# Order of a few steps in the RWKV-7 and sparse-attention stages of a decoder-layer kernel

## The reference, cut to what matters

```python
def step(S, inp):
    r_t, w_t, k_t, v_t, kk_t, a_t = inp
    sa = jnp.einsum('bhij,bhj->bhi', S, -kk_t)
    S = (S * w_t[:, :, None, :] + sa[..., None] * (kk_t * a_t)[:, :, None, :]
         + v_t[..., None] * k_t[:, :, None, :])
    return S, jnp.einsum('bhij,bhj->bhi', S, r_t)
...
_, sel = lax.top_k(index, topk)
...
logits = jnp.einsum('bthd,btkhd->bthk', q, k_sel).astype(jnp.float32) * HEAD_DIM ** -0.5 + bias
```

## Time and profile before

| | us |
|---|---|
| median of 3 runs | 1629.0 |
| lowest and highest | 1625.16, 1631.47 |
| the profiled execution: its own time | 1633.64 |
| its span on the engines | 1631.9 |
| TensorE matmul busy | 1535.6 |
| VectorE busy | 1140.8 |
| ScalarE busy | 730.0 |
| GpSimd busy | 269.3 |

### The profile page before, as it was taken

One profiled execution on the slowest core, in us unless ns is written; L12 is line 12 of the kernel. 1 busy time (PEld: TensorE's weight loads), 2 busy tenths in 40 slices (PEclk: granted clock), 3 DMA queues, 4 the chain that ended last, 5 costly groups with the idle time before them and its releaser, 6 DMA issues.

```text
span 1631.9 us, 41517 instructions
## 1 busy us (share of the span) xinstructions
PE 1535.6 (94%) x17667; PEld 1197.5 (73%) x17667; DVE 1140.8 (70%) x2453; ACT 730.0 (45%) x1286; POOL 269.3 (17%) x188
## 2 busy tenths in 40 slices
PE   6999999999999797899779999999999999999998
PEld 4586666664667576677657976888888888888887
DVE  3699999988767756877632789988888886100056
ACT  4743232113678555666553224555555554311100
POOL 2422111012211111212123000000000002322100
PEclk9999999998999798998999999999999999999999
DMA  8223122325530203000105211111222222821001
GB/s 300 62 79 131 53 71 71 101 92 167 158 105 21 73 10 125 23 23 23 56 11 189 90 45 52 53 53 53 83 101 79 79 92 94 319 78 53 27 30 79
DMA packets 53874, 138.84 MB, mean 85 GB/s; under 512 B 17594, under 2 KB 24506, under 8 KB 46362
## 3 DMA queue, kind: packets, MB, share of 16 engines
q1 hardware_dynamic: 52602, 135.13, 24.3%
q0 software_dynamic: 1088, 1.05, 0.2%
HBM read 106.44 MB, written 29.72 MB: 83 GB/s over the span
## 4 chain that ended last, share of the span: by engine, by line
PE 82%; DVE 9%; issue 3%; ACT 3%; SPq 2%; DMA 1%; DVEq 0%; ACTq 0%
PE bank L2618 78%; PE bank L2785 2%; DVE arena L3001 1%; DVE arena L2281 1%; PE bank L1079 1%; SPq L972 1%; PE bank L1024 1%; DVE arena L2315 0%; DMA arena<-oht 0%; PE bank L1984 0%; SPq L831 0%; DVE arena L1650 0%; SPq L835 0%; DVE arena L2999 0%; DVE arena L2293 0%
## 5 line engine op out<-in xcount | busy, mean ns | idle before, releaser
L2618 PE MATMUL bank<-arena 64*64 64x64 f32 (+11 forms) x16960 | 1452.4, 278 | 83.9 <-issue 18.2
L2618 PEld LDWEIGHTS bank<-arena 128*128 128x128 f16 (+7 forms) x16960 | 1120.5, 120 | 413.8 <-issue 125.8
L3041 DVE TENSOR_SCALAR_CACHE_REDUCE arena<-arena 128x384 bf16<-128x384 f32 (+6 forms) x231 | 196.9, 916 | 1.2
L3170 POOL TENSOR_TENSOR arena<-arena 128x2048 f16<-128x2048 f32 x32 | 130.3, 4074 | 398.4 <-ACT arena L2828 386.2
L2827 ACT ACTIVATE arena<-arena 128x2048 f16<-128x2048 f32 x32 | 61.0, 1906 | 160.7 <-PE bank L2618 134.4
L2844 ACT ACTIVATE arena<-bank 128x352 f32<-128x352 f32 x72 | 33.1, 462 | 183.9 <-PE bank L2618 183.9
L1831 POOL TENSOR_TENSOR arena<-arena 128x512 f32<-128x512 f32 x40 | 54.4, 1367 | 241.9 <-PE bank L2618 107.9
L2475 POOL COPY arena<-arena 128x2 f32<-128x2 f32 x22 | 22.4, 1019 | 426.5 <-DVE arena L2415 326.7
L2446 DVE COPY arena<-bank 128x256 f32<-128x256 f32 x4 | 1.7, 424 | 121.5 <-PE bank L2618 121.5
L2138 ACT ACTIVATE arena<-arena 128x1024 f16<-128x1024 f32 x76 | 65.9, 938 | 35.7 <-DVEq L2306 35.7
L2193 ACT ACTIVATE arena<-bank 128x264 f32<-128x264 f32 x114 | 43.4, 389 | 79.0 <-PE bank L2618 79.0
(11 more groups left out here) (290 smaller groups left out, 1431.8 us busy)
## 6 DMA issues: line engine op xcount, KB each, us to landing
arena<-slabs SPq DMA_DIRECT2D x53, 1024.0 KB, 4.9
arena<-kcache SPq DMA_DIRECT2D x32, 256.0 KB, 2.9
arena<-vcache SPq DMA_DIRECT2D x32, 256.0 KB, 2.9
prw<-arena SPq DMA_DIRECT2D x42, 176.0 KB, 1.9
hd<-arena SPq DMA_DIRECT2D x11, 528.0 KB, 2.7
arena<-xt SPq DMA_DIRECT2D x8, 528.0 KB, 11.3
x1d<-arena SPq DMA_DIRECT2D x8, 512.0 KB, 2.6
arena<-x1d SPq DMA_DIRECT2D x1, 4096.0 KB, 19.1
```

What stands on the lines that cost most here:

```text
L2618: return nc.tensor.matmul(out, lhsT, rhs, start=start, stop=stop, skip_group_check=True)
L3041: last = dve.tensor_scalar(junk, a, s, None, op, ALU.add, accum_out=cnt[:, k:k + 1])
L3170: pool.tensor_tensor(WL[r].rearrange("p a b -> p (a b)"), STG[s], WH[r].rearrange("p a b -> p (a b)"), ALU.subtract).then_inc(slab_lo, 1)
```

## The change

Five edits. (1) In `RW_PERIOD`, `lx` of level 3 (item k-2) stands ahead of `fin` 0 (item k-1) where it stood behind it. (2) The sample steps of periods 1 and 2 are placed later: `zscan`, `zsquare` with `zln`, and `zkm` each move behind the neighbouring level step, `zexp` and `zbo` go behind `lp` 3 of period 2, and `zfin` behind `lx` 3. (3) `zout` moves from behind `lx` 1 of period 2 to behind `bo` of period 3, and the 16 stores on SP from behind the raw transfer of item 2 to behind that of item 3. (4) The mask of query block 7 is made in two pieces, three instructions at `svalues` 0 and two at `svalues` 1; that of block 6 stays. (5) SP reads the 16 page numbers of a round into registers ahead of the wait for that round's buffers, and the loop that issues the transfers uses these registers.

```diff
+MASK_STEPS = {("slogits", 0): (6, range(5)), ("svalues", 0): (7, range(3)), ("svalues", 1): (7, range(3, 5))}
...
-    ("exp", "a", 1), ("norm", "a"), ("lp", "b", 3), ("km", "a"), ("ch", "c", 1), ("rstd", "d"), ("split", "t", 1), ("fin", "a", 0), ("lx", "b", 3),
+    ("exp", "a", 1), ("norm", "a"), ("lp", "b", 3), ("km", "a"), ("ch", "c", 1), ("rstd", "d"), ("split", "t", 1), ("lx", "b", 3), ("fin", "a", 0),
...
-    ("zgate", "z0"), ("bv", "a"), ("y", "c"), ("split", "s", 0), ("ch", "c", 7), ("out", "c", 0), ("lp", "a", 1), ("ss", "p"), ("zscan", "z0"),
-    ("ln", "p"), ("cen", "c"), ("out", "c", 1), ("lx", "a", 1), ("scan", "p"), ("gh", "b"), ("zsquare", "z0"), ("zln", "z0"), ("var", "c"),
-    ("out", "c", 2), ("lp", "a", 2), ("exp", "p", 0), ("zkm", "z0"), ("ry", "b"), ("ch", "b", 0), ("lx", "a", 2), ("zbo", "z0"), ("zexp", "z0"))
-RW_SAMPLE = {(2, "lp", 3): ("zfin",), (2, "bo"): ("ztl",), ...
-             (2, "lx", 1): ("zout",), (2, "gh"): ("zvar",), ...
+    ("zgate", "z0"), ("bv", "a"), ("y", "c"), ("split", "s", 0), ("ch", "c", 7), ("out", "c", 0), ("lp", "a", 1), ("ss", "p"),
+    ("ln", "p"), ("cen", "c"), ("out", "c", 1), ("lx", "a", 1), ("zscan", "z0"), ("scan", "p"), ("gh", "b"), ("var", "c"),
+    ("out", "c", 2), ("lp", "a", 2), ("zsquare", "z0"), ("zln", "z0"), ("exp", "p", 0), ("ry", "b"), ("ch", "b", 0), ("lx", "a", 2), ("zkm", "z0"))
+RW_SAMPLE = {(2, "lp", 3): ("zexp", "zbo"), (2, "lx", 3): ("zfin",), (2, "bo"): ("ztl",), ...
+             (3, "bo"): ("zout",), (2, "gh"): ("zvar",), ...
...
-                if n == 2:
+                if n == 3:
                     emptied(sp, ("zout", 0, HP - 1))
...
+        def page_numbers(sp, r):
+            at = [PG * (4 * (r % 2) + q) + g for q in range(4) for g in range(PG)]
+            return [sp.value_load(PTB[0:1, n:n + 1], min_val=0, max_val=NPOOL - 1) for n in at]
...
             for r, read in enumerate((("slg", 0, 0), ("slg", 1, 0), ("sav", 0))):
+                pages = page_numbers(sp, r + 1)
                 sp.wait_ge(filled, plan.number(read) + 1)
                 for q in range(4):
-                    load_pages(sp, r + 1, q)
+                    load_pages(sp, r + 1, q, pages)
...
-                if kind == "slogits":
-                    for n in range(5):
-                        mask(LATE_MASKS[u] - 2, n, MASKTMP)
-                    dve.sem_inc(mask_ready, 1)
+                if (kind, u) in MASK_STEPS:
+                    j, steps = MASK_STEPS[kind, u]
+                    for n in steps:
+                        mask(j - 2, n, MASKTMP)
+                    if n == 4:
+                        dve.sem_inc(mask_ready, 1)
```

More of the change, by code:

```diff
@@ L2599, in _ @@
                     sp.wait_ge(pt_in, 16)
+                    pages = page_numbers(sp, 0)
                 if w >= SL_OUT - NRING:
[L2601 removed]
+                    load_pages(sp, 0, w % NRING, pages)
             for q in range(4):
```

10 lines of the change are left out of this document (4 added, 6 removed).

## The result

The changed kernel takes 1619.2 us (median of 7 runs, 1614.5 to 1621.4) against 1629.0 us (7 runs, 1625.2 to 1631.5): a ratio of 0.9936, 95% interval 0.9921 to 0.9950, which is 10.4 us less, between 8.1 and 12.9. The forecast was 1612 us, 17 us less, in a range of 1605 to 1620. So the sign and the range held, and the gain came out at six tenths of what the sum promised. Its profiled execution took 1621.4 us, with a span of 1619.7.

A forecast was written before the change was run, and what follows sets the result against it. PE, busy for 94% of the span, was taken as the bound, so only its waits or lower clock could be won. Terms 2.8 + 1.6 + 2.3 - 0.1 + 4.2 + 5.2 + 1.2 = 17.2 us gave 1612 us, range 1605 to 1620.

The forecast's parts named there:

- Pages: Attention, ahead of `svalues` 1: PE's wait for value pages goes, 2.8 us, or 0 if the transfers were the limit.
- The term for the clock: At `svalues` 1, behind the page wait: PE's work at the lower clock returns to the higher, 1.6 us, bounds 0 and 1.6.
- Mask: Attention, unit 10: PE's wait for DVE shrinks by 2.3 us (bounds 1.7 and 3.3), less 0.1 charged behind `svalues` 0.
- Turn to period 2: Recurrence, sample steps regrouped and edit 1: level 4 of item 0 starts 4.2 us earlier, bounds 2.6 and 5.
- Stores and period 3: Edit 3, and edit 1 in period 3: 3.26 us raw-transfer wait plus 2.0 us at `zout`; 5.2 us, bounds 3.3 and 6.
- Swap in periods 4 to 8: Edit 1 ahead of level 4: 0.9 us kept in period 6, 0.3 in period 5; 1.2 us, bounds 0 and 3.6.
- DVE takes it back: Rival: in the recurrence PE then waits for DVE at the next `ch`, `fin` or `km`; 10.4 us gain, 1619; chance 0.18.
- The clock gives more: Rival: fewer waits keep PE at the higher clock in the recurrence, 5 us in its first half; 1606; chance 0.08.
- the case of the lower bounds: Rival "Nothing measurable": transfers bound round 3 and ACT the turn, leaving 6.6 us, 1622; chance 0.08.
- The test that I had set myself: Recurrence, 530 to 865 us: prediction wrong if granted clock changes by more than 0.05 or the stretch shrinks under 8 us.

The follow-up runs named there:

- small_pool: Changed kernel with GpSimd's masking products of levels 3 to 5 cut to one of eight pairs, so the recurrence is not computed: 0.9919 of the kernel before.
- swap: Kernel before with edit 1 alone (level update ahead of `fin` 0): 0.9974 of the kernel before, 4.2 us less.
- no_stores: Changed kernel with edit 3 undone (`zout` and the 16 stores back ahead of the raw transfer of item 3): 0.9941 of the kernel before.
- stores: Kernel before with edit 3 alone (`zout` and the 16 state stores moved behind the raw transfer of item 3): 1.0003 of the kernel before.

## Why the prediction was right in sign and too large in size

**Pages: the wait right, the clock not.** The wait is gone, and SP issues its 16 transfers of round 3 in 9.5 us, 0.59 us apart (forecast 0.63). SP's timeline of the changed kernel and PE's at `svalues` 1:

```profile
435.23 9.49 SPq L840 DMA_DIRECT2D arena<-vcache  x16
...
451.87 7.79 PE L2625 MATMUL bank<-arena 64*128 64x256 f32 x74
```

The transfers kept up. The term for the clock, 1.6 us, is where this step failed: the lower level did leave `svalues` 1, but it came only in three of five traces with the wait, and all eight kernels with edit 5 have it behind a later wait instead, where the same 42 matmuls take 5.6 us or more in place of 4.09. Net of that the term is about nothing. Alone the edit gained 4.9 us (2.6 to 7.3), so the total does not contradict it.

**Mask: right in total, by another split.** The units up to 14 came 2.8 us earlier in six of the kernels with this edit, for a forecast of 2.3 less 0.1. Only 1.2 us of it is idle time, about half of what was forecast, and 1.6 us is PE's clock behind the wait, which the term had only in its upper bound. That the two make up the 2.3 us is partly luck. Only the changed kernel and `small_pool` have 1.1, because their `slogits` 1 ran at the lower clock. PE's wait in unit 10 is 1.44 us in place of 2.34, not below 0.7 as announced. And 0.7 us is given back behind `svalues` 0, seven times the 0.1 charged:

```profile
414.72 1.29 PE L2625 MATMUL bank<-arena 128*64 128x128 f32 x14 [1.44 <-issue]
...
438.26 1.36 PE L2625 MATMUL bank<-arena 64*128 64x256 f32 x12 [0.71 <-DVE arena L3161]
```

The second place had been named (softmax scaling behind the first pieces), within its bounds of 0 and 1.0. The first piece took 5.0 us (432.76 to 437.79), between the 5.4 and the 4.3 that the prediction had for it, since a product of GpSimd (432.31 to 433.60) ran beside its first instruction here, too. Both attention edits together give 4.8 to 4.9 us at `sm` 0 in five of the kernels, for 6.6 in the sum: what is missing is about the 1.6 of clock.

**Turn to period 2: mis-sized, 3.4 in place of 4.2 us.** Level 4 of item 0 starts 18.0 us behind PE's first row after `sm` 0 (538.79 to 556.76), for 21.4 before (543.38 to 564.76). The wait of 3.09 us ahead of level 4 fell to 0.79, and the other waits on the way, 4.5 us in four before, are 4.5 us in five now. So waits give 2.3 of the 3.4 us; the rest is PE's clock, 0.85 in place of 0.79 from `sm` 0 to `xi` 1. PE's timeline and then DVE's and GpSimd's:

```profile
549.48 1.11 PE L2625 MATMUL bank<-arena 128*128 128x128 f32 x34 [1.02 <-DVE arena L1742]
...
553.52 0.49 PE L2625 MATMUL bank<-arena 128*128 128x128 f32 x2 [1.05 <-DVE arena L1753]
555.20 0.77 PE L2625 MATMUL bank<-arena 64*64 64x64 f32 x32 [1.19 <-ACT arena L1433]
556.76 1.13 PE L2625 MATMUL bank<-arena 64*64 64x64 f32 x32 [0.79 <-DVE arena L1655]
...
547.71 0.29 DVE L1741 TENSOR_TENSOR arena<-arena 128x128 f32<-128x128 f32 x1
548.03 1.40 DVE L1742 TENSOR_TENSOR arena<-arena 128x128 f32<-128x128 f32 x1
...
552.23 1.24 DVE L1753 TENSOR_TENSOR arena<-arena 128x128 f32<-128x128 f32 x1
...
548.01 1.27 POOL L1836 TENSOR_TENSOR arena<-arena 128x512 f32<-128x512 f32 x1 [3.12 <-PE bank L2625]
552.03 1.30 POOL L1836 TENSOR_TENSOR arena<-arena 128x512 f32<-128x512 f32 x1 [2.74 <-PE bank L2625]
```

I had followed the chain "with the durations of today". But the regrouped sample steps came to lie beside GpSimd's masks, and two instructions that take 0.29 us alone took 1.40 and 1.24, each to within 0.2 us of the end of the mask's product beside it; both are the ones for which PE then waited. Of the 4.2 us I had given to both edits, the swap alone brings 2.0 in its trace.

**Stores and period 3: the step that failed.** The sum took the wait for the raw transfer, 3.26 us, and 2.0 us at `zout` as PE's to win, 5.2 us, and the edit measured as nothing (1.0003, and `no_stores` equal to the changed kernel). The stretch to `xi` 2 did shrink by 6.2 us, but 2.3 of it came back before `xi` 3. The raw wait was read from a single execution, in which it was the longest of the six traces with the old order. And of the steps that were moved I followed the transfers of the recurrence to their readers, but not what the load of x, next in the queue, does to the others: it has slack for its own reader, as the text said, and on its way it holds back PE's instructions: the wait there is 3.43 us in place of 2.08. Of other kernels with edit 3 `stores` has 3.8 us there in two waits.

**Swap in periods 4 to 8: near zero, and its reason right.** The 1.2 us rested on periods in which PE is at the lower clock. The wait of 0.5 us in place of 1.45 ahead of level 4 is there. The longer one at `ch` is 1.24 in place of 0.85, and 0.93 us ahead of `tl` 0, which I had not named, takes the rest; the 0 that the prediction gave to periods 4 and 8 was the right answer for all of them. The total of `swap` alone, 4.2 us, is not explained by this.

**The rivals.** "DVE takes it back" had forecast 1619 and had the mechanism for periods 4 to 8 right, but it kept 3.3 us for edit 3, which brought none. "The clock gives more" had a part too: it gave some 4.6 of the 10.4 us, and without it the waits alone, some 6 us, would have come near the case of the lower bounds, 6.6 us. The upper bounds add up to 22.3 us, not 22.5, which changes nothing. So a time of 1619 was reached by two errors of opposite sign, terms for waits that were two to three times too large and a clock that helped. That it fell inside the range owes something to luck. The test that I had set myself, a change of the clock of over 0.05 from 530 to 865 us, was not met: it rose by 0.04 and 0.05 in the two windows. The other was, just: I had called myself wrong if the recurrence shrank by less than 8 us, and it shrank by 7.6 (PE's first row of the late stage stood at 864.39 and is now at 852.15, 12.2 us earlier, of which 4.6 were won ahead of `sm` 0).

## What to carry over

Before a wait is counted as won, look for it in more than one execution, and for the same edit ask how much work each of the two engines has between this meeting point and the next: if the later one's list from here to there is longer, the order within the list is worth nothing. A large load is not free because its reader is far away: it can hold back the transfers of PE's own instructions. Moved as a whole it moved the wait; whether a place in which PE runs long instructions would hide it no run tried. And a sum of PE's waits should be held against PE's idle time between two fixed instructions, together with the granted clock there, since idle time also falls when PE runs slower.

## What the runs showed of the hardware

- PE can stand still for its own instructions. In thirteen traces 88 waits with the cause "issue" stand 193 or 194 records behind a multiple of 256, with exactly as many 16 KB transfers of queue 8 landed, the last one 1.2 to 1.6 us earlier. With the DMA engines full of a 2.6 MB load the wait at one such place was 3.4 us; with the load moved away two waits of 1.9 us in all remained, and one of 2.2 us stood where the load now was.
- A DVE instruction beside a GpSimd product of 1.27 to 1.42 us takes about 0.9 to 1.1 us more, a short one as much as a longer one (0.29 to 1.40, 0.75 to 1.64 us), and it is back at 0.75 in all eight items when the product is cut to one eighth.
- The mean granted clock of a run of this kernel varied between 0.968 and 0.979 for the kernel before alone (60 runs), and each 0.001 goes with 0.7 us. The same wait for pages was followed by the lower level in three of five traces. In all eight traces without that wait the lower level stood at a later one, where only one of the five has it. So a cost of clock read behind one wait in one trace is not a saving that removing the wait can be counted on to bring.
